# Leaving the empty slots out of a gather of expert rows

## Chip, cores and metric

The kernel runs on one core of one Trainium2 chip. Times are device microseconds (us) of one launch; the figure compared is the median of several runs of the same kernel. "MB" is a million bytes.

## The reference

One transformer-like block over 512 tokens of 2048 float32 features: a layer norm, a token mixer (eight gated DeltaNet heads beside a sliding-window attention) with one input and one output projection, a second layer norm, a mixture of experts, and a last layer norm. The change lies in the mixture of experts, which is

```
eid      = the 2 experts of each token            # of 32, inside one of 4 groups
weights  = p(group) * renormalised top-2 probability
for each expert e, for the tokens that chose it:
    hdn = silu(x @ w_gate[e]) * (x @ w_up[e])     # 2048 -> 512
    y[token] += weight * (hdn @ w_down[e])        # 512 -> 2048
```

512 tokens with two choices each make 1024 rows over 32 experts, 32 for an expert on average. Evaluating the reference on its inputs gives these counts, for experts 0 to 31: 35 47 27 28 38 35 31 35 25 10 21 26 41 40 27 16 23 24 29 31 29 48 26 32 46 34 41 41 37 26 43 32. None is over 64, and 14 of them are over 32.

## The kernel before

The first 1100 us or so compute the projections and the mixer. Then the second layer norm leaves 512 rows `r1` in SBUF, which ACT also stores to `h1_scr` in HBM, and PE makes router logits (semaphore `logits`, 2 when both parts are there).

**Routing table.** DVE works out, step by step (semaphore `rt`), where each of the 1024 choices goes in a table in HBM, `slot_rows`: 512 places for each expert, of two numbers each, a token's index and a weight. At the very start of the program POOL has filled the whole table with zeros from the tile `unused` (line 557, 559). Later POOL writes the choices into it with eight scatters (line 615), and when they have landed it reads the first `SLOTS` = 64 places of each expert into `idx_all`, twice, once for each half of the partitions (line 622). A place that no choice has filled keeps index 0 and weight 0, so it stands for token 0 with weight 0.

**Gather.** For each of the 32 experts ("block" t), POOL issues one indirect DMA (line 629), which fetches 64 rows of `h1_scr`, 8 KB each, one for each slot, into half of the tile `xb`: partitions 0 to 63 for even t and 64 to 127 for odd t. Slot s goes to partition s of the half. From t = 2 on it waits until PE has transposed the rows of block t - 2 (`xT_ps`), so at most two gathers are ahead. The tile `xb` shares its memory with `h1T`, which the router's matmuls read until `logits`.

**Weights.** An expert has 12 pieces of 1 MB (1.049 million bytes): 8 of gate and up, 4 of down. SP loads them on its own queue (line 532) into a ring of 15 slots, each as soon as PE is done with what lay there (`w_used`). The first 14 are loaded before the routing is known.

**Expert.** PE transposes the gathered rows (line 1873), multiplies with gate and up (line 1897), then with down (line 1906); ACT scales the result with the slots' weights (line 945), and PE adds it to the tokens' rows through a 0/1 matrix `place`, which DVE makes by comparing each token's number with the slots' indices `tok_all` (line 1478, PE line 1866, DVE line 1448). PE runs the combining matmuls of block t - 1 between the gate and up matmuls of block t.

Rows beyond 64 of an expert would go through a loop at the end (`left`); with the counts above it has nothing to do.

Of the kernel before, what the change touches and what calls it, by code (L numbers as in the profile page):

```python
# [32 lines left out]
S = 512  # L33
# [17 lines left out]
SLOTS = 64  # L51
# [56 lines left out]
def build(nc, x, ln0_g, ln0_b, w_in, conv_w, a_log, dt_bias, gdn_norm_w, sinks, w_o, ln1_g, ln1_b,  # L108
# [11 lines left out]
    with ctx:  # L120
        def sem(name):
            return ctx.enter_context(nc.semaphore(name))
# [16 lines left out]
        def at(name, offset, shape, dt=F32):  # L139
            size = 4 * int(np.prod(shape[1:]))  # L140
            assert offset + size <= ARENA, (name, offset + size)
            placed[name] = offset + size
            return nc.alloc_sbuf_tensor_at(name, list(shape), dt, offset=base + offset)
# [19 lines left out]
        o = GD  # L163
# [39 lines left out]
        xb = at("xb", GD + 24 * KB, [P, D])  # L203
# [10 lines left out]
        o = CN  # L214
        small = {}

        def keep(name, shape, dt=F32):
            nonlocal o
            t = at(name, o, shape, dt)
            o += (4 * int(np.prod(shape[1:])) + 31) // 32 * 32  # L220
            return t
# [28 lines left out]
        idx = keep("idx", [P, 2], I32)  # L250
        idx_all = at("idx_all", GD + 47 * KB, [P, E, 2], I32)
# [32 lines left out]
        unused = at("unused", MX, [P, 2 * E * CAP // P], I32)  # L284
# [80 lines left out]
        gathered = [sem(f"gathered{i}") for i in range(2)]  # L365
# [15 lines left out]
        def W(eng, s, n):  # L381

            if not (isinstance(n, int) and n <= 0):
                eng.wait_ge(s, n)
# [33 lines left out]
        def slot(j):  # L418

            return (1 + j) % 2  # L420
# [133 lines left out]
        @block.gpsimd  # L554
        def _(pool):

            pool.memset(unused[:, :], 0).then_inc(table_zeroed, 1)
            pool.wait_ge(table_zeroed, 1)
            pool.dma_start(slot_rows.rearrange("(p n) o -> p (n o)", p=P), unused[:, :]).then_inc(table_zero, 16)
            pool.memset(eps[:, 0:1], LN_EPS).then_inc(zero_pad, 1)  # L560
            pool.memset(eps[:, 1:2], RMS_EPS).then_inc(zero_pad, 1)
            def lo(s, sl):
                pool.wait_ge(strip_hi, s + 1)
                W(pool, strip_mm, s - 1)
                pool.tensor_tensor(wlo[sl][:, :, :].rearrange("p k n -> p (k n)"), raw[sl][:, :],  # L565
                                   whi[sl][:, :, :].rearrange("p k n -> p (k n)").bitcast(F32),
                                   ALU.subtract).then_inc(strip_lo, 1)

            lo(0, 0)
            lo(1, 1)  # L570

            def iteration(it, gdn=True, last=False):
                for j in range(4):
                    lo(4 * it + 2 + j, slot(j + 1))
                    if j == 1 and not gdn:

                        pool.wait_ge(h_stored, 16 * TT)
                        for i in range(3):
                            pool.memset(xp[i][:, 0:CONV - 1], 0.0).then_inc(zero_pad, 1)
                    if j == 0 and gdn:  # L580

                        pool.wait_ge(par_done, 1)
                        pool.wait_ge(dec_exp, it)
                        ed = T["Ed"][:, :].rearrange("p (c i) -> p c i", c=TT)
                        pool.affine_select(out=ed, in_=ed, compare_op=ALU.is_ge, fill=0.0, base=0,
                                           pattern=[[0, TT], [-1, P]], channel_multiplier=1).then_inc(dec, 1)
                        if last:
                            for i in range(3):
                                pool.wait_ge(silu[i], HEADS)
                            pool.memset(kdup[:, :, 0:P], 0.0).then_inc(kpad, 1)  # L590

            iteration(0, gdn=False)
            with pool.Fori(1, HEADS) as it:
                iteration(it)
            iteration(HEADS, last=True)
            with pool.Fori(0, 4) as m:
                for j in range(2):
                    lo(2 * m + (Q0 + 1 + j), j)
            with pool.Fori(0, 3) as nt:
                for kg_ in range(4):  # L600
                    lo(4 * nt + (O0 + 1 + kg_), kg_ % 2)
            for kg_ in range(3):
                lo(O0 + 13 + kg_, kg_ % 2)

            pool.wait_ge(ld_ln1, 80)
            pool.wait_ge(l1_norm, TT)
            pool.tensor_tensor(r1[:, TT - 1, :], r1[:, TT - 1, :], g1[:, :], ALU.mult).then_inc(h1_last, 1)
            pool.wait_ge(h1_last, 1)
            pool.tensor_tensor(r1[:, TT - 1, :], r1[:, TT - 1, :], b1[:, :], ALU.add).then_inc(h1_last, 1)

            pool.wait_ge(table_zero, 16)
            pool.wait_ge(rt, RT_DEST)
            for t in range(TT):
                for c in range(2):
                    pool.indirect_dma_start(slot_rows, bass.IndirectOffsetOnAxis(ap=rd[:, t, c:c + 1], axis=0),
                                            toki[:, t, c, :], None).then_inc(scattered, 16)
            pool.wait_ge(scattered, 16 * 2 * TT)
            pool.wait_ge(rt, RT_ALL)
            pool.wait_ge(logits, 2)
            pool.wait_ge(h1_stored, 16 * TT)  # L620
            for h in range(2):
                pool.dma_start(idx_all[SLOTS * h:SLOTS * (h + 1), :, :],
                               slot_rows.rearrange("(e c) o -> c e o", c=CAP)[0:SLOTS, :, :]).then_inc(scattered, 16)
            pool.wait_ge(scattered, 16 * 2 * TT + 32)
            for t in range(E):
                half_ = slice(SLOTS * (t % 2), SLOTS * (t % 2 + 1))
                if t >= 2:
                    pool.wait_ge(xT_ps, 2 * (t - 1))
                pool.indirect_dma_start(xb[half_, :], None, h1_scr,  # L629
                                        bass.IndirectOffsetOnAxis(ap=idx_all[0:SLOTS, t, 0:1], axis=0)).then_inc(gathered[t % 2], 16)  # L630

            r_idx = pool.alloc_register("r_idx")
            left = pool.value_load(ovi[0:1, 2 * LEFTOVER:2 * LEFTOVER + 1], min_val=0, max_val=LEFTOVER)
            with pool.If(left > 0):
                with pool.Fori(0, left) as i:
                    row = pool.value_load(ovi[0:1, bass.ds(i + LEFTOVER, 1)], min_val=0, max_val=E * CAP - SLOTS)
                    pool.wait_ge(lf_dve, LF_DVE * i + LF_START)
                    for h in range(2):
                        pool.dma_start(idx[SLOTS * h:SLOTS * (h + 1), :], slot_rows[bass.ds(row, SLOTS), :]).then_inc(lf_rows, 16)
                    pool.reg_mov(r_idx, 48 * i + 32)  # L640
                    pool.wait_ge(h1_stored, 16 * TT)
                    pool.wait_ge(lf_rows, r_idx)
                    pool.indirect_dma_start(xb[0:SLOTS, :], None, h1_scr,
                                            bass.IndirectOffsetOnAxis(ap=idx[0:SLOTS, 0:1], axis=0)).then_inc(lf_rows, 16)

            pool.wait_ge(ld_ln2, 32)
            for i, t in enumerate(POOL_TILES):
                pool.wait_ge(f_root, 2 + i)
                pool.tensor_tensor(r1[:, t, :], r1[:, t, :], b2[:, :], ALU.add).then_inc(f_done_p, 1)
# [1348 lines left out]
```

## Time and profile before

| | |
|---|---|
| median of 3 runs (lowest, highest) | 2295.27 us (2295.11, 2295.28) |
| profiled execution, its own time | 2295.32 us |
| its span in the profile | 2293.5 us |
| mean granted TensorE clock | 0.933 of full speed |
| bytes read from HBM, written | 499.92 MB, 12.72 MB |
| busy: PE, DVE, ACT, POOL | 85%, 52%, 27%, 15% of the span |

The span is what the engines' records cover; the profiled execution's own time is 1.8 us longer. An engine's busy share is an average over very different stages, so the stage around the change is read by itself.

### The profile page before, as it was taken

Reading aid. Unit: us, or ns where it says so; the run is one execution under the profiler, and the core shown is the slowest. Engines: PE = TensorE matmul, PEld = TensorE weight load, DVE = VectorE, ACT = ScalarE, POOL = GpSimd, SP = SyncE. Lnnn points to the kernel's source line nnn. Section 1 sums busy time; section 2 is a strip of 40 time slices with the busy share of each in tenths; the row PEclk is TensorE's granted clock in tenths of the full one; section 3 lists DMA queues with packets and bytes.
Section 4 is the critical chain, followed back from the end, with each engine's and each line's share of the span. In section 5 each row is a group of like instructions: output and inputs, shape, how many; then the busy total and the mean of one; then the engine's idle time right before and its main releaser. Section 6 shows DMA issues by size and latency. Waiting matters only on the chain.

```text
span 2293.5 us, 24624 instructions
## 1 busy us (share of the span) xinstructions
PE 1950.0 (85%) x9654; PEld 1218.4 (53%) x9654; DVE 1182.2 (52%) x1772; ACT 615.4 (27%) x915; POOL 355.3 (15%) x128
## 2 busy tenths in 40 slices
PE   4899999999998987899619998889889888988991
PEld 3677787778777765688513433333333333333330
DVE  6777557656664355310523554454445444544558
ACT  4224313322332354311321222212221222122211
POOL 1422222221322212144320000000000000000002
PEclk8999999999999898899869999999999999999995
DMA  5422212112212211432558999999999999999991
GB/s 182 149 72 55 55 37 73 45 47 55 69 47 56 56 55 55 139 110 91 202 154 331 392 404 395 394 394 407 391 395 402 398 394 394 407 393 391 407 392 74
DMA packets 168958, 513.75 MB, mean 224 GB/s; under 512 B 13393, under 2 KB 105745, under 8 KB 114353
## 3 DMA queue, kind: packets, MB, share of 16 engines
q1 hardware_dynamic: 165344, 491.53, 56.5%
q0 software_dynamic: 2960, 16.95, 3.2%
q10 hardware_dynamic: 576, 4.19, 0.4%
q8 instruction: 54, 0.88, 0.2%
q14 instruction: 24, 0.19, 0.0%
HBM read 499.92 MB, written 12.72 MB: 224 GB/s over the span
## 4 chain that ended last, share of the span: by engine, by line
PE 46%; DMA 30%; DVE 14%; issue 4%; ACT 3%; SPq 2%; POOL 0%; DVEq 0%; ACTq 0%
DMA ring<-in_w_up 27%; PE bank L1897 8%; PE bank L1559 7%; PE bank L1560 7%; PE bank L1561 7%; PE bank L1906 3%; PE bank L1866 2%; PE bank L1690 2%; PE bank L1687 2%; DVE half L1091 2%; PE bank L1679 2%; SPq L532 2%; DMA ring<-in_w_down 1%; DVE gd_L L1212 1%; DVE sc L1264 1%
## 5 line engine op out<-in xcount | busy, mean ns | idle before, releaser
L1897 PE MATMUL bank<-ring,xbT 128*64 128x512 f32 x2048 | 507.9, 641 | 92.5 <-DMA ring<-in_w_up 91.6
L1448 DVE TENSOR_TENSOR r<-r,bank 128x512 f32<-128x512 f32 x512 | 318.1, 681 | 249.9 <-PE bank L1866 248.1
L565 POOL TENSOR_TENSOR wlo<-raw,whi 128x2048 fp32r<-128x2048 f32 x61 | 283.1, 4641 | 700.4 <-ACT whi L678 474.1
L1897 PEld LDWEIGHTS bank<-ring,xbT 128*64 128x64 f32 x2048 | 158.0, 146 | 393.7 <-issue 392.7
L1559 PE MATMUL bank<-hTh,wlo 128*128 128x512 f32 x720 | 309.0, 429 | 20.3 <-POOL wlo L565 14.3
L1560 PE MATMUL bank<-hTl,whi 128*128 128x512 f32 x720 | 285.4, 396 | 0.0
L1561 PE MATMUL bank<-hTh,whi 128*128 128x512 f32 x720 | 285.2, 396 | 0.0
L945 ACT ACTIVATE yw<-bank,wts_all 64x512 f32<-64x512 f32 x256 | 174.8, 683 | 253.2 <-PE bank L1906 249.1
L1906 PE MATMUL bank<-ring,hidT 128*64 128x512 f32 x1024 | 227.0, 595 | 2.3 <-DMA ring<-in_w_down 1.8
L629 POOL DMA_INDIRECT xb<-h_scr,idx_all x32 | 28.8, 898 | 917.8 <-PE bank L1873 907.3
L1866 PE MATMUL bank<-yhl,place 128*128 128x512 f32 x512 | 158.2, 429 | 13.0 <-DVE r L1448 10.1
L1559 PEld LDWEIGHTS bank<-hTh,wlo 128*128 128x128 f32 x720 | 139.3, 193 | 47.2 <-issue 20.4
L1453 DVE CAST yhl<-yw 128x512 fp32r<-128x512 f32 x128 | 53.8, 421 | 200.0 <-ACT yw L945 200.0
L934 ACT ACTIVATE hid<-bank 64x512 f32<-64x512 f32 x32 | 18.9, 589 | 509.5 <-PE bank L1897 509.5
L1561 PEld LDWEIGHTS bank<-hTh,whi 128*128 128x128 f32 x720 | 137.8, 191 | 31.0
L1560 PEld LDWEIGHTS bank<-hTl,whi 128*128 128x128 f32 x720 | 139.1, 193 | 21.7 <-issue 0.7
L1906 PEld LDWEIGHTS bank<-ring,hidT 128*64 128x64 f32 x1024 | 70.6, 137 | 142.0 <-issue 138.7
L678 ACT ACTIVATE whi<-raw 128x2048 fp32r<-128x2048 f32 x53 | 101.1, 1907 | 165.3 <-PE bank L1561 165.2
L1866 PEld LDWEIGHTS bank<-yhl,place 128*128 128x128 f32 x512 | 87.5, 190 | 108.6 <-issue 89.8
L1559 PE MATMUL bank<-whi,mxl 128*128 128x512 f32 x256 | 100.5, 392 | 0.7 <-ACT mixT L845 0.7
L1560 PE MATMUL bank<-wlo,mxh 128*128 128x512 f32 x256 | 100.3, 392 | 0.0
L1561 PE MATMUL bank<-whi,mxh 128*128 128x512 f32 x256 | 100.2, 391 | 0.0
(299 smaller groups left out, 2219.9 us busy)
## 6 DMA issues: line engine op xcount, KB each, us to landing
ring<-in_w_gate SPq DMA_DIRECT2D x128, 1024.0 KB, 29.8
ring<-in_w_up SPq DMA_DIRECT2D x128, 1024.0 KB, 30.3
ring<-in_w_down SPq DMA_DIRECT2D x128, 1024.0 KB, 29.1
raw<-in_w_in SPq DMA_DIRECT2D x45, 1024.0 KB, 5.5
raw<-in_w_o SPq DMA_DIRECT2D x16, 1024.0 KB, 5.1
xt<-in_x SPq DMA_DIRECT2D x4, 1024.0 KB, 9.3
h_scr<-xt SPq DMA_DIRECT2D x4, 1024.0 KB, 4.3
r<-h_scr SPq DMA_DIRECT2D x1, 4096.0 KB, 13.8
```

The source lines that it names most:

```text
L532: sp.dma_start(ring[n % RING][:, :], weight_source(t, i)).then_inc(w_loaded[n % RING], 16)
L565: pool.tensor_tensor(wlo[sl][:, :, :].rearrange("p k n -> p (k n)"), raw[sl][:, :], whi[sl][:, :, :].rearrange("p k n -> p (k n)").bitcast ...
L678: act.activation(whi[sl][:, :, :].rearrange("p k n -> p (k n)"), raw[sl][:, :], ACT.Copy).then_inc(strip_hi, 1)
L945: i = act.activation(yw[half_, q, :], DN[j][SLOTS * h:SLOTS * (h + 1), :], ACT.Copy, scale=wts_all[half_, t:t + 1])
L1448: dve.tensor_tensor(v, v, comb_bank(q, tt)[:, :], ALU.add).then_inc(comb_done, 1)
L1453: dve.tensor_copy(yhl[:, q, :], yw[:, q, :]).then_inc(yw_split, 1)
L1559: mm(bank, lo_, rh, start=first, stop=False)
L1560: mm(bank, hi_, rl, start=False, stop=False)
L1561: return mm(bank, hi_, rh, start=False, stop=final)
L1866: mm(comb_bank(q, tt)[:, :], place[n % 2][:, tt * P:(tt + 1) * P], yhl[:, q, :], start=True, stop=True).then_inc(comb_ps, 1)
L1897: i = mm(GU[SLOTS * h:SLOTS * (h + 1), :], xT_[:, k, :], w[:, kk * F:(kk + 1) * F], start=k == 0, stop=k == KD - 1)
L1906: i = mm(DN[j][SLOTS * h:SLOTS * (h + 1), :], hidT[:, c, :], w[:, n0:n0 + F], start=c == 0, stop=c == KF - 1)
```

## The change

The table starts with index `S` = 512 in every place, one past the last token, in place of 0 (the weight stays 0); this takes two memsets with a stride in place of one. The gather of rows (and the one of the loop at the end) gets a bound: an index over `S` - 1 = 511 is left out and is no error. Such a slot's partition of `xb` then keeps what lay in it, so POOL sets the whole tile `xb` to zero once, after `logits` has reached 2 and before it waits for the scatters. `place` has no 1 for index 512, since the tokens are numbered 0 to 511. How many rows an expert has is known only on the chip, so the matmuls still work on 64 slots.

```diff
-            pool.memset(unused[:, :], 0).then_inc(table_zeroed, 1)
-            pool.wait_ge(table_zeroed, 1)
+            fields = unused[:, :].rearrange("p (n o) -> p n o", o=2)
+            pool.memset(fields[:, :, 0:1], S).then_inc(table_zeroed, 1)
+            pool.memset(fields[:, :, 1:2], 0).then_inc(table_zeroed, 1)
+            pool.wait_ge(table_zeroed, 2)
             pool.dma_start(slot_rows.rearrange("(p n) o -> p (n o)", p=P), unused[:, :]).then_inc(table_zero, 16)
...
                     pool.indirect_dma_start(slot_rows, bass.IndirectOffsetOnAxis(ap=rd[:, t, c:c + 1], axis=0),
                                             toki[:, t, c, :], None).then_inc(scattered, 16)
+            pool.wait_ge(logits, 2)
+            pool.memset(xb[:, :], 0.0).then_inc(table_zeroed, 1)
             pool.wait_ge(scattered, 16 * 2 * TT)
             pool.wait_ge(rt, RT_ALL)
-            pool.wait_ge(logits, 2)
+            pool.wait_ge(table_zeroed, 3)
             pool.wait_ge(h1_stored, 16 * TT)
...
                 pool.indirect_dma_start(xb[half_, :], None, h1_scr,
-                                        bass.IndirectOffsetOnAxis(ap=idx_all[0:SLOTS, t, 0:1], axis=0)).then_inc(gathered[t % 2], 16)
+                                        bass.IndirectOffsetOnAxis(ap=idx_all[0:SLOTS, t, 0:1], axis=0),
+                                        bounds_check=S - 1, oob_is_err=False).then_inc(gathered[t % 2], 16)
...
                     pool.indirect_dma_start(xb[0:SLOTS, :], None, h1_scr,
-                                            bass.IndirectOffsetOnAxis(ap=idx[0:SLOTS, 0:1], axis=0)).then_inc(lf_rows, 16)
+                                            bass.IndirectOffsetOnAxis(ap=idx[0:SLOTS, 0:1], axis=0),
+                                            bounds_check=S - 1, oob_is_err=False).then_inc(lf_rows, 16)
```

Between the scatters and the first gathers, POOL's program reads like this before the change (the number is the row's place in POOL's program; `x7` stands for seven alike; the waits are those added since the row above):

```order
68 L615 DMA slot_rows<-toki,rd 16384x2 [waits rt,table_zero]
69 L615 DMA slot_rows<-toki,rd 16384x2 x7
70 L622 DMA idx_all<-slot_rows 64x32x2 [waits logits,h1_stored,rt,scattered]
71 L622 DMA idx_all<-slot_rows 64x32x2
72 L629 DMA xb<-h_scr,idx_all 64x2048 [waits scattered]
73 L629 DMA xb<-h_scr,idx_all 64x2048
74 L629 DMA xb<-h_scr,idx_all 64x2048 [waits xT_ps] x30
```

And like this after it, in the lines of the changed kernel:

```order
69 L617 DMA slot_rows<-toki,rd 16384x2 [waits rt,table_zero]
70 L617 DMA slot_rows<-toki,rd 16384x2 x7
71 L620 MEMSET xb 128x2048 [waits logits]
72 L626 DMA idx_all<-slot_rows 64x32x2 [waits table_zeroed,h1_stored,rt,scattered]
73 L626 DMA idx_all<-slot_rows 64x32x2
74 L633 DMA xb<-h_scr,idx_all 64x2048 [waits scattered]
75 L633 DMA xb<-h_scr,idx_all 64x2048
76 L633 DMA xb<-h_scr,idx_all 64x2048 [waits xT_ps] x30
```

One memset has come in between the scatters and the reading of the table, and the wait on `logits` has moved to it. PE, DVE, ACT and SP keep their instructions and their order.

## Rows read from the trace of the kernel before

**Rows 1.** The page: the span in 40 equal slices (57.3 us each).

```profile
DMA  5422212112212211432558999999999999999991
GB/s 182 149 72 55 55 37 73 45 47 55 69 47 56 56 55 55 139 110 91 202 154 331 392 404 395 394 394 407 391 395 402 398 394 394 407 393 391 407 392 74
```

**Rows 2.** The page: DMA queues; packets, MB, share of 16 engines' span.

```profile
q1 hardware_dynamic: 165344, 491.53, 56.5%
q0 software_dynamic: 2960, 16.95, 3.2%
```

**Rows 3.** Waits of PE from 1200 us on: total, times, longest.

```profile
PE bank L1897 <- DMA ring<-in_w_up: 91.6, 52, 4.5
PE bank L1873 <- DMA xb<-h_scr,idx_all: 42.0, 1, 42.0
```

**Rows 4.** The chain that ended last, in order of time: start, us, what.

```profile
1178.26 9.90 DMA slot_rows<-toki,rd
...
1200.87 5.61 DMA xb<-h_scr,idx_all
1206.53 2.03 PE bank L1873 x16
...
1285.17 7.02 PE bank L1906 x32
...
1312.78 7.02 PE bank L1906 x32
...
2195.96 27.00 DMA ring<-in_w_up
2223.10 3.67 PE bank L1897 x16
```

**Rows 5.** Line 629 before 1215 us and from 1339 us: durations in ns, starts, landing.

```profile
L629 POOL DMA_INDIRECT xb<-h_scr,idx_all x3: 901/924/933, 1200.9 to 1208.8; - x3
...
L629 POOL DMA_INDIRECT xb<-h_scr,idx_all x25: 892/896/902, 1339.5 to 2136.4; - x25
DMA to landing us min/median/max: 9.0/9.5/10.3
```

**Rows 6.** Stretches: us, PE, PEld, DVE, ACT, POOL busy, PEclk, DMA share, GB/s.

```profile
1202.00:1206.00 4.00, 0.00 (x0) 0.00 (x0) 0.00 (x0) 0.00 (x0) 0.92 (x1) 0.50 0.89 203
1222.00:1232.00 10.00, 8.59 (x51) 4.15 (x48) 1.87 (x3) 2.85 (x4) 0.89 (x1) 1.00 1.01 425
1428.00:1442.00 14.00, 14.00 (x74) 6.59 (x74) 10.16 (x17) 1.57 (x3) 0.90 (x1) 1.00 1.01 421
1443.90:1447.90 4.00, 3.72 (x18) 1.01 (x14) 0.00 (x0) 0.23 (x1) 0.00 (x0) 1.00 1.05 260
1410.00:2210.00 800.00, 714.75 (x3198) 287.05 (x3196) 382.55 (x650) 172.11 (x269) 19.72 (x22) 0.95 1.01 398
2212.00:2222.00 10.00, 9.63 (x42) 3.88 (x40) 7.07 (x13) 0.20 (x1) 0.00 (x0) 1.00 1.02 421
```

**Rows 7.** POOL in order of time: start, busy us, instruction, idle before it.

```profile
1178.26 0.97 POOL L615 DMA_INDIRECT slot_rows<-toki,rd  x1 [0.30 <-issue]
1188.45 2.27 POOL L622 DMA_DIRECT2D idx_all<-slot_rows  x2 [9.22 <-DMA slot_rows<-toki,rd]
1202.11 0.92 POOL L629 DMA_INDIRECT xb<-h_scr,idx_all  x1 [0.30 <-issue]
```

**Rows 8.** POOL by line: count, busy us, mean ns, idle before.

```profile
L565 POOL TENSOR_TENSOR wlo<-raw,whi 128x2048 fp32r<-128x2048 f32 x61 | 283.1, 4641 | 700.4 <-ACT whi L678 474.1 <-ACT whi L686 226.3
L590 POOL MEMSET kdup<- 128x512 f32 x1 | 0.5, 524 | 0.0
```

**Rows 9.** The page: DMA issues; count, KB each, us to landing.

```profile
xt<-in_x SPq DMA_DIRECT2D x4, 1024.0 KB, 9.3
```

## The prediction

> **What bounds the kernel now.** I read the page's slices first. From about the 23rd slice of 40 to the 39th, some 980 us, the DMA row says 9 (over 90% of all 16 engines) at 391 to 407 GB/s, while before that it is mostly 1 to 5 [rows 1]. That stretch is the mixture of experts, and its 384 pieces of weights make 403 MB. Then the stretches: in the 800 us from 1410 us on the DMA share is 1.01 and the rate 398 GB/s [rows 6]; it is 1.01 already at 1222 to 1232 us and still 1.02 at 2212 to 2222 us. So the DMA engines have work without a gap for 1000 us, and what the transfers take there is what the stage takes. PE's waits agree: 91.6 us for `ring<-in_w_up`, 52 times; the next in size, 42.0 us, is the one wait for the first gather [rows 3]. The chain ends with a load that lands at 2223 us and then PE's last gate and up matmuls [rows 4], after which comes a tail that the change does not touch. PE could go faster: early on, with a full ring, two blocks' down matmuls start at 1285.17 and 1312.78 us, 27.6 us apart [rows 4], whereas the gathers from 1339.5 to 2136.4 us, which are 25 and so 24 blocks, come 796.9 / 24 = 33.2 us apart [rows 5].
>
> **What a gather costs.** This is the number that the case turns on. Of the loads alone the rate is 421 GB/s (1428 to 1442 us, and again at the end) [rows 6]. Twelve pieces of 1.049 MB at that rate are 12.58 / 0.421 = 29.9 us. The block takes 33.2 us, so one gather of 64 rows costs the loads 3.3 us. By its bytes it should cost 0.524 MB / 0.421 = 1.25 us. The rest is seen in the 4 us of a gather: the rate falls to 260 GB/s, the gather's own bytes included, at a DMA share of 1.05 [rows 6]. All engines are busy and move less. The gather writes to 64 of the 128 partitions only, and the first two gathers, which run with nothing beside them, show the same: 203 GB/s at a share of 0.89, half of 421 [rows 6]. So rows bound for half of the partitions go in at half the rate, and loads that share an engine with them are held up behind them.
>
> The Trainium skill (DMA: Bandwidth & Descriptors, Anatomy of one DMA) prices a transfer on this path at about 2.0 us fixed, which overlaps with others, plus its bytes over 436e3 per us: for one gather an estimate of 1.2 us of engine time, and 0.6 us saved by halving it, 17 us over 29 gathers. The rows say 3.3 us per gather, and halving that would be 48 us; I go by the rows.
>
> **The change part by part.**
>
> *Rows left out.* 1024 of 2048 rows stay [the counts with the reference]: 8.4 of the 16.95 MB of the software queue go [rows 2]. Of the 32 gathers the first three are issued before the loads fill the engines again (by 1208.8 us [rows 5]; the DMA share is full from 1222 us); the other 29 lie in the saturated stretch, and each us that they cost less is a us off the end, as long as PE's 27.6 us per block stays below the DMA's time. Even with nothing left of a gather that is 29.9, so it does.
>
> How much one gather gets cheaper depends on who carries the rows that stay. The filled slots are the first ones of the 64, since choices are numbered from 0 in each expert. The share of 0.89 with nothing but gathers on the queues [rows 6] says that all 16 engines carry rows, so four each. The loads give every engine the same amount, each load is complete only when all 16 are, so what counts is the most burdened engine. Two ways to deal the rows:
> - In order, four successive slots to an engine. The first engine has slots 0 to 3, which are filled for every expert, and the engines up to the seventh have nearly all of theirs. Their own work, 4 rows of 8 KB at 421 / 16 = 26.3 GB/s, 1.25 us, stays in full. What can go is the other 3.3 - 1.25 = 2.05 us, which came from two rows meeting at one place. Half of the rows are gone, so half of that, 1.0 us; and in the 14 of 32 experts with over 32 rows there is still a second row to meet for the first engines, which I count as no gain: 1.0 x 18/32 = 0.58 us per gather.
> - Spread, so that every engine loses half of its rows. Then half of 3.3 us goes, 1.65 us per gather.
>
> No view of the trace says which engine takes which slot, since every row is 8 KB whether filled or not. I take the first, as the plainest way to cut a list of 64 into 16 shares: 29 x 0.58 = 16.8 us. The ends are 0 and 29 x 3.3 / 2 = 48 us.
>
> The Trainium skill speaks for the first (same page, Why a DMA increments its semaphore by 16: SWDGE puts ceil(partitions/16) successive partitions on each engine for some direct copies, so that 100 partitions leave the last engine without data). It speaks of direct copies, and no row here shows it for an indirect one.
>
> *First gather.* It is on the chain: 5.61 us from 1200.87 us, then PE's transposes [rows 4]. 0.524 MB at 203 GB/s are 2.6 us of it. With 35 rows, four on an engine and alone at 26.3 GB/s, that is 1.25 us, so PE starts 1.3 us earlier, and the loads behind it too. The check of 64 indices could cost something: the gather's instruction takes 0.92 us now [rows 7]; a doubling would eat 0.9 of it. I take 1.3 us, with 0 and 2 as ends.
>
> *The memset of `xb`.* 128x512 took 524 ns on POOL, so at most four times that, 2.1 us, for 2048 columns; a subtraction of that size takes 4.64 us, the upper end [rows 8]. It comes after the last scatter, which ends at 1179.23 us, and POOL idles 9.22 us there until the scatters land [rows 7]. So it costs nothing; without that cover it would put 2.1 us on the chain, once. `logits` has long been at 2, since the scatters themselves need the routing that follows it.
>
> *The two strided memsets* at the start replace one of the same 256 columns (under 0.524 us by the row of 512 [rows 8]), and the table is needed only 1100 us later: nothing. The two `eps` memsets behind them go a fraction of a us later, and ACT needs them only when rows of x have landed, which takes 9.3 us [rows 9], and been summed.
>
> *The bound on later gathers* could lengthen their instructions, but POOL idles for most of 33 us before each, and a gather lands 9.5 us after its issue [rows 5], one block ahead of its use.
>
> **Sum.** Against the profiled execution's own 2295.32 us, 0.05 us above the median: 2295.3 - 16.8 - 1.3 = 2277.2 us.
>
> **The rivals.**
> - *The rows spread evenly over the engines.* For it: no row excludes it, and a rule that looks at the slot's number some other way than by runs of four is easy to imagine. Against it: nothing but that cutting the list into 16 runs is the simplest. 2295.3 - 48 - 1.3 = 2246 us, and up to 2262 if only part is even. Chance 0.22.
> - *Nothing is saved, because the change doesn't leave transfers out*: a slot over the bound is given a transfer of its own all the same, to some other place. For it: no row of this trace has a bounded gather. 2295.3 us, or 2294 if the first gather is a little shorter. Chance 0.12.
> - *Slower: the uneven load pulls the engines apart.* The first engines fall behind at each gather and the others run ahead until the ring's 15 pieces stop them; if the rows of the first engines then meet loads of engines that never pause for rows of their own, each row waits longer than now (8 KB at 260 / 16 = 16.3 GB/s are 0.50 us, against 0.31 us undisturbed). At a third more per gather, 1.1 us x 29 = 32 us, it would be 2295.3 + 32 - 1.3 = 2326 us; it decides once the first engines' cost is over the present 3.3 us. Against it: half of the writers to the crowded half have gone. Chance 0.05.
> - *The forecast*, 2266 to 2290 us: 0.61.
>
> The Trainium skill (same page, The descriptor swizzle) gives 128-partition transfers an engine by (partition >> 2) & 7 within 64 partitions; by that alone a 64-partition gather would lie on 8 engines, with slots s and s + 32 on the same, and skipping would relieve each. The share of 0.89 with gathers alone speaks against it here.
>
> **Numbers.** From the chances: 0.8 of the mass lies between 2251 us, into the spread case, and 2291 us, short of no change. About 0.2% (4.6 us) is what a measurement of this kernel can tell from no change. Faster by more than that: the forecast, the spread case, and a little of the third: 0.86; within it 0.09; slower 0.05.
>
> **What would show it.** In the changed profile: the software queue at some 8.6 MB in place of 16.95; 24 blocks from the eighth gather's issue on at 32.6 us each in place of 33.2; the rate in the 4 us of a gather above 260 GB/s; PE's wait for `ring<-in_w_up` down by about 15 us; and the DMA share a little below 1.01, since half of the engines have less to do. If the share stays at 1.01 and the blocks come at 31.5 us, the rows were spread. If the bytes are as before, the bound did nothing. I would be wrong upwards if PE, not the loads, took over the chain; PE at 27.6 us per block says that it does not.

## The result, and the profile after

The changed kernel takes 2255.12 us (median of 4 runs, 2253.01 to 2259.62) against 2295.28 us (2295.11 to 2296.24): a ratio of 0.9829, 95% interval 0.9816 to 0.9842, so 40 us or 1.7% off, well outside the noise. The profiled execution took 2253.29 us. I had forecast 2277.2 us.

The page of the changed kernel: the slices (56.3 us each), and the DMA queues, to be read against [rows 1, 2].

```profile
DMA  5422112112211221243266999999999999999991
GB/s 186 149 76 56 41 52 63 48 53 59 56 49 52 75 57 37 86 150 103 105 277 195 406 406 406 409 410 403 407 406 415 401 410 402 409 399 401 413 377 75
...
q1 hardware_dynamic: 165344, 491.53, 57.2%
q0 software_dynamic: 2960, 8.57, 1.7%
```

The stage is as saturated as it was, at mostly 399 to 415 GB/s in place of 391 to 407, and 8.4 MB less of it is gathered rows. The software queue moves 8.57 MB in place of 16.95, as it should, and its share of the engines' time has fallen from 3.2 to 1.7%. Its packets are still 2960: a left-out row of 8 KB has become a packet of 4 bytes (in the packet records 1024 of each size have changed places). The page's "HBM read" stays at 499.92 MB before and after, and at 499.92 MB in e2 below, which gathers nearly nothing, so it does not count these packets.

The waits of PE in the stage (to be read against [rows 3]):

```profile
PE bank L1903 <- DMA ring<-in_w_up: 71.2, 66, 4.3
PE bank L1879 <- DMA xb<-h_scr,idx_all: 39.5, 1, 39.5
```

The chain that ended last, in order of time (against [rows 4]):

```profile
1176.46 8.28 DMA slot_rows<-toki,rd
1185.03 1.15 POOL idx_all L626
1186.18 10.97 DMA idx_all<-slot_rows
1197.95 4.27 DMA xb<-h_scr,idx_all
1202.27 2.02 PE bank L1879 x16
...
2154.60 26.35 DMA ring<-in_w_up
```

From the landing of the first gather to the landing of the last load of gate and up, the last one on the chain, it was 2195.96 + 27.00 - 1200.87 - 5.61 = 1016.5 us, and is 2154.60 + 26.35 - 1197.95 - 4.27 = 978.7 us. That is 37.8 us, by far the most of the change. The first gather also lands 4.3 us earlier (1202.22 against 1206.48 us). Of these, 1.34 are its own (5.61 to 4.27); the rest comes from the scatters before it, their start and their landing, and moves as much in kernels that don't touch them (in e1 below the first gather starts at 1201.79 us, in e5 at 1198.80).

Lines 633 and 620 on POOL, in order of time, then line 633's gathers as a group, to be read against [rows 5, 7]:

```profile
1177.43 1.82 POOL L620 MEMSET xb<- 128x2048 f32 x1
1185.03 2.27 POOL L626 DMA_DIRECT2D idx_all<-slot_rows  x2 [5.78 <-DMA slot_rows<-toki,rd]
...
1394.64 0.93 POOL L633 DMA_INDIRECT xb<-h_scr,idx_all  x1 [26.66 <-PE bank L1879]
1426.79 0.94 POOL L633 DMA_INDIRECT xb<-h_scr,idx_all  x1 [31.22 <-PE bank L1879]
1456.97 0.93 POOL L633 DMA_INDIRECT xb<-h_scr,idx_all  x1 [29.24 <-PE bank L1879]
```

```profile
L633 POOL DMA_INDIRECT xb<-h_scr,idx_all x24: 931/935/939, 1367.0 to 2097.1; - x24
DMA to landing us min/median/max: 7.4/7.9/9.3
```

The memset takes 1.82 us and POOL still idles 5.78 us behind it. A gather's instruction is 0.04 us longer than before (0.935 against 0.896), which lies in POOL's idle time. The blocks come (2097.1 - 1367.0) / 23 = 31.7 us apart in place of 33.2, and a gather lands after 7.9 us in place of 9.5.

Stretches of the changed kernel (columns as in [rows 6]): the 4 us after two gathers reach the DMA engines, with 21 and 26 rows, and 760 us of the stage.

```profile
1430.90:1434.90 4.00, 3.27 (x16) 0.86 (x12) 0.00 (x0) 0.68 (x1) 0.00 (x0) 1.00 1.01 346
1461.00:1465.00 4.00, 3.59 (x18) 1.00 (x14) 0.00 (x0) 0.36 (x1) 0.00 (x0) 1.00 1.01 311
1410.00:2170.00 760.00, 691.05 (x3169) 283.71 (x3170) 381.43 (x648) 167.90 (x263) 20.56 (x22) 0.98 1.01 407
```

The rate during a gather falls to 346 and 311 GB/s where it fell to 260. The share is still 1.01: on average no engine has time without a packet in the middle of the stage. The prediction had named blocks of 31.5 us at a share of 1.01 as the sign that the rows were spread, and blocks of 32.6 us for its own case; 31.7 us is the former.

### The profile page after: what moved, and what is told of

It reads as the page before. It is cut to its first block, busy times and chain, and to the rows that moved or that the text cites. A ratio compares the mean times of both kernels' runs of the same rounds, so it can differ in the third digit from the quotient of the medians.

```text
span 2251.5 us, 24658 instructions
## 1 busy us (share of the span) xinstructions
PE 1932.4 (86%) x9654; PEld 1215.6 (54%) x9654; DVE 1183.3 (53%) x1772; ACT 615.2 (27%) x915; POOL 360.1 (16%) x130
## 3 DMA queue, kind: packets, MB, share of 16 engines
q0 software_dynamic: 2960, 8.57, 1.7%
HBM read 499.92 MB, written 12.72 MB: 228 GB/s over the span
## 4 chain that ended last, share of the span: by engine, by line
PE 46%; DMA 31%; DVE 15%; issue 4%; ACT 3%; SPq 1%; POOL 1%; DVEq 0%; ACTq 0%; POOLq 0%
DMA ring<-in_w_up 29%; PE bank L1903 8%; PE bank L1565 7%; PE bank L1566 7%; PE bank L1567 7%; PE bank L1912 3%; PE bank L1696 2%; PE bank L1872 2%; PE bank L1693 2%; PE bank L1685 2%; DVE half L1097 2%; DVE gd_L L1218 1%; DVE sc L1270 1%; SPq L532 1%; PE bank L1645 1%
## 5 line engine op out<-in xcount | busy, mean ns | idle before, releaser
L1903 PE MATMUL bank<-ring,xbT 128*64 128x512 f32 x2048 | 488.1, 620 | 72.6 <-DMA ring<-in_w_up 71.2
L1872 PE MATMUL bank<-yhl,place 128*128 128x512 f32 x512 | 159.2, 431 | 12.1 <-DVE r L1454 9.2
```

Source lines behind the costliest of these rows:

```text
L1872: mm(comb_bank(q, tt)[:, :], place[n % 2][:, tt * P:(tt + 1) * P], yhl[:, q, :], start=True, stop=True).then_inc(comb_ps, 1)
L1903: i = mm(GU[SLOTS * h:SLOTS * (h + 1), :], xT_[:, k, :], w[:, kk * F:(kk + 1) * F], start=k == 0, stop=k == KD - 1)
```

## The experiments

Theory P, formed after the result: the rows that stay are spread over the engines more evenly than I had assumed, because an engine does not take four successive slots but two pairs, slots 2e, 2e + 1 and 32 + 2e, 33 + 2e for engine e. It came from the start times of the software queue's 8 KB packets in the trace of the changed kernel. Theory F is the prediction's, four successive slots. For the gather of expert 9, which has 10 rows, these are the starts of its packets in us from the gather's issue, read from the packet records, with two later kernels beside it that are described below:

```
changed kernel  4.19 4.27 4.29 4.34 4.35 | 4.97 5.17 5.24 5.37 5.38
by fours (e9)   4.35 4.39 4.41 | 4.71 5.18 5.25 | 6.21 6.38 | 7.21 7.52
one by one(e10) 4.23 4.24 4.26 4.28 4.30 4.32 4.33 4.34 4.35 4.39
```

In the changed kernel five rows start together and five more some 0.9 us later: five engines with two rows each. By theory F it would be three engines, with four, four and two. That is what e9 shows, which was built to deal choices so: groups of 3, 3, 2 and 2. In e10, built to give every row its own engine, all ten start within 0.16 us. (The bars are mine. A row takes 0.31 us where nothing disturbs it, so there is room for a packet of the loads before the engine's next row.)

The diffs below are cut to what matters; counts in waits that change with them are left out.

**The memset alone (e1).**

```diff
+            pool.wait_ge(logits, 2)
+            pool.memset(xb[:, :], 0.0).then_inc(table_zeroed, 1)
             pool.wait_ge(scattered, 16 * 2 * TT)
             pool.wait_ge(rt, RT_ALL)
-            pool.wait_ge(logits, 2)
+            pool.wait_ge(table_zeroed, 2)
```

> The kernel before with nothing added but the memset of xb between the scatters and the reading of the table. Every theory: the memset (1.82 us in the changed kernel) lies in the 9.2 us that POOL idles there, so no change, 2295.3 us within 1. If it weren't hidden, 2297.

Measured: 2295.49 us (10 runs), ratio 0.9998 (0.9986 to 1.001). The interval reaches from -3.2 to +2.3 us, which by itself would not exclude the memset's 1.8 us. The trace of e1 does: POOL idles 6.54 us behind the memset until the scatters have landed, so it is hidden.

```profile
1180.95 1.82 POOL L618 MEMSET xb<- 128x2048 f32 x1
1189.32 2.28 POOL L624 DMA_DIRECT2D idx_all<-slot_rows  x2 [6.54 <-DMA slot_rows<-toki,rd]
```

**All rows left out (e2).**

```diff
-                                        bounds_check=S - 1, oob_is_err=False).then_inc(gathered[t % 2], 16)
+                                        bounds_check=0, oob_is_err=False).then_inc(gathered[t % 2], 16)
```

> The changed kernel with the bound at 0, so that all rows but those of token 0 are left out (the experts then work on zeros for the others). Theory A, a left-out slot costs the DMA engines nothing: the block falls from 31.7 us to the 29.9 us of its loads alone, 29 x 1.8 = 53 us off the changed kernel, about 2202 us. Theory B, an empty slot still costs an engine a turn: with 4 on each engine at, say, 0.1 us, the block stays at 30.3 us, about 2214 us.

Measured: 2202.02 us (2201.47 to 2202.84), ratio 0.9592 (0.9576 to 0.9609). Theory A holds: a left-out slot costs the engines nothing that can be seen. Its page shows the stage at the rate of loads alone:

```profile
GB/s 190 153 77 39 57 57 57 57 38 66 48 41 81 39 65 50 39 182 96 76 281 83 400 421 420 420 420 421 421 421 421 420 421 420 421 421 420 421 380 76
DMA packets 168957, 497.00 MB, mean 226 GB/s; under 512 B 15438, under 2 KB 107790, under 8 KB 116398
...
q0 software_dynamic: 2960, 0.20, 0.4%
```

This kernel is the floor for the rest: what the others take above 2202.0 us, over 29 gathers, is what a gather costs. For the kernel before it is (2295.3 - 2202.0) / 29 = 3.2 us, close to the 3.3 us of the prediction, which was read from the blocks' distance. (The kernels' starts differ too, and that is in it. The first gather lands at 1202.25 us in e2 and at 1206.48 in the kernel before, which makes 0.15 us per gather. By the stage alone, from that landing to the landing of the last load of gate and up, 926.9 us in e2 and 1016.5 before, a gather costs 3.1 us.)

**Two dealings of 32 rows (e3, e4).** Both have the same number of rows, the same bytes and the same groups of four partitions; only the engines differ, if theory P is right. The diff is that of e3; e4 has `(0, 1)` in place of `(0, 2)`.

```diff
-            pool.memset(fields[:, :, 0:1], S).then_inc(table_zeroed, 1)
+            pool.memset(fields[:, :, 0:1], 0).then_inc(table_zeroed, 1)
...
+            pool.memset(idx_all[:, :, :], S).then_inc(table_zeroed, 1)
...
             for h in range(2):
-                pool.dma_start(idx_all[SLOTS * h:SLOTS * (h + 1), :, :],
-                               slot_rows.rearrange("(e c) o -> c e o", c=CAP)[0:SLOTS, :, :]).then_inc(scattered, 16)
+                for first in (0, 2):
+                    pool.dma_start(idx_all[SLOTS * h + first:SLOTS * (h + 1):4, :, :],
+                                   slot_rows.rearrange("(e c) o -> c e o", c=CAP)[first:SLOTS:4, :, :]).then_inc(scattered, 16)
```

> Exactly 32 rows in every gather: the table starts with index 0 as before, but idx_all is preset to the index out of bounds and only slots 0, 2, 4, ... 62 of each expert are loaded into it (choices in odd places are left out of the result; two more small DMAs in the start, some 2 us). Theory P, an engine has slots 2e, 2e+1, 32+2e and 33+2e: two rows on every engine, half of the 3.3 us go in 29 gathers, 2295.3 - 48 - 1.3 + 2.3 = 2248 us. Theory F, an engine has four successive slots: two rows on every engine too, the same 2248 us.

> As the one with even slots, and again exactly 32 rows in every gather, but slots 0, 1, 4, 5, 8, 9, ... 60, 61. Theory P: eight engines have four rows and the other eight none; the loads wait for the eight, as in my forecast for four successive slots, so 0.6 to 1 us less than 3.3 per gather, 2268 to 2279 us. Theory F: two rows on every engine, as with the even slots, 2248 us.

Measured: 2245.05 us (2243.03 to 2245.39), ratio 0.9776 (0.9758 to 0.9794), for the even slots; 2269.19 us (2268.47 to 2270.36), ratio 0.9884 (0.9867 to 0.9902), for the paired ones. 24 us between them with equal bytes: theory F, which gives both the same, falls. A gather costs 1.5 us with two rows on every engine, and 2.3 us with four on eight engines. Both figures flatter a little: the reading of the table lands after 4.62 us in these two in place of 11, so the first gather lands at 1198.1 us, 4 us earlier than in e2, where I had added 2.3 us. By the stage alone (974.9 and 998.9 us against 926.9) it is 1.7 and 2.5 us, and the difference of 24 us stays. How the loads end shows the engines pulled apart. Paired slots:

```profile
2185.00:2195.00 10.00, 9.64 (x42) 3.91 (x41) 7.08 (x13) 0.38 (x1) 0.00 (x0) 1.00 0.86 357
2195.00:2205.00 10.00, 6.91 (x32) 2.74 (x32) 5.86 (x11) 0.98 (x2) 0.00 (x0) 1.00 0.46 192
2205.00:2211.00 6.00, 5.76 (x28) 1.72 (x24) 0.96 (x2) 0.19 (x1) 0.00 (x0) 1.00 0.19 78
```

Even slots:

```profile
2165.00:2175.00 10.00, 9.62 (x44) 3.90 (x41) 7.07 (x13) 0.00 (x0) 0.00 (x0) 1.00 1.02 421
2175.00:2185.00 10.00, 8.59 (x42) 3.26 (x40) 4.29 (x8) 0.97 (x2) 0.00 (x0) 1.00 0.71 295
```

With the paired slots some half of the engines are done 10 us and more before the others (a share of 0.46 over 10 us, then 0.19); with the even slots the share is full until nearly the end. (The last transfers are the two parameter rows of the last layer norm, dealt to all engines alike.) The loads' semaphores say the same. Each rises in sixteen steps, which I take for the sixteen engines' shares. These are the steps of the very last weight load, in us from its first step, read from the semaphore records:

```
even (e3)    0.0 0.2 0.7 0.8 0.9 2.6 2.9 5.4 6.0 6.4 6.4 6.8 6.8 6.9 8.7 9.4
paired (e4)  0.0 0.1 0.2 0.2 0.3 0.9 1.6 1.6 | 11.2 11.3 12.1 13.7 17.1 17.4 17.8 19.9
```

Eight steps come within 1.6 us, and the other eight 11 to 20 us after the first: eight engines against eight, as theory P has it. Over the middle of the stage (loads from 1500 to 2100 us) the median distance from the first step to the sixteenth is 5.2 us in e2, 5.8 in the kernel before, 6.4 with the even slots, 8.8 in e10, 13.2 in the changed kernel, and 21.0 with the paired slots and in e9. What is read as a wait for `ring<-in_w_up` is a wait for the fullest engine's part of it.

**Dealt by fours, and one by one (e9, e10).** Here all rows are gathered, and the order in which the table's places are loaded into the slots is changed so that, by theory P, an engine gets four successive choices (e9), or choice j goes to engine j modulo 16 (e10). The diff is that of e9; e10 reads places `32 * c + 16 * b` to `32 * c + 16 * b + 15` in the last line.

```diff
             for h in range(2):
-                pool.dma_start(idx_all[SLOTS * h:SLOTS * (h + 1), :, :],
-                               slot_rows.rearrange("(e c) o -> c e o", c=CAP)[0:SLOTS, :, :]).then_inc(scattered, 16)
+                for c in range(2):
+                    for b in range(2):
+                        pool.dma_start(idx_all[SLOTS * h + 32 * c + b:SLOTS * h + 32 * c + 32:2, :, :],
+                                       slot_rows.rearrange("(e c) o -> c e o", c=CAP)[2 * c + b:SLOTS:4, :, :]).then_inc(scattered, 16)
```

> The changed kernel, all rows gathered, but the table's places are loaded into the slots in an order that gives each DMA engine (by theory P) four successive choices, which is what my prediction assumed: the first engine then has 128 of the run's 1024 rows. Six more small DMAs of 1.15 us at the start, some 7 us on the chain. Theory P: the prediction's sum for this dealing, 2277, plus 7, so 2275 to 2284 us. If it isn't the fullest engine that decides, as in the changed kernel plus 7: 2262 us.

> The same with the same DMAs at the start, but choice j goes to a slot of engine j modulo 16 (by theory P), so the fullest engine has 76 of 1024 rows in place of 92 in the changed kernel. Theory P: somewhat less than the changed kernel plus 7, 2252 to 2260 us, and about 20 us less than dealt by fours. If the dealing doesn't matter: both kernels the same.

Measured: 2289.12 us (10 runs, 2284.13 to 2292.68), ratio 0.9976 (0.9967 to 0.9986), by fours; 2250.65 us (2249.7 to 2251.41), ratio 0.9813 (0.9796 to 0.9829), one by one. 38 us between two kernels that do the same transfers. The 7 us that I had added for more DMAs at the start were wrong: the two parts of the chain, issue and landing, add up to the same. Without them the range for e10 would have been 2245 to 2253 us, and it lies there; whether it is faster than the changed kernel's 2255.1 us is left open by the two intervals, which overlap. The chain by fours:

```profile
1185.87 4.43 POOL idx_all L628 x7
1190.31 6.94 DMA idx_all<-slot_rows
1198.08 5.27 DMA xb<-h_scr,idx_all
```

4.43 + 6.94 = 11.4 us, against 1.15 + 10.97 = 12.1 in the changed kernel. So e9, 5 us over the range that I had given for it, is 12 us over its top once those 7 us are taken off (2268 to 2277), and that matters: a gather costs (2289.1 - 2202.0) / 29 = 3.0 us there, hardly less than the 3.2 of 64 full rows. Two 4 us stretches of its gathers, with 21 and 26 rows:

```profile
1438.30:1442.30 4.00, 3.29 (x16) 0.86 (x12) 0.00 (x0) 0.66 (x1) 0.00 (x0) 1.00 1.02 297
1471.50:1475.50 4.00, 3.62 (x18) 1.01 (x14) 0.00 (x0) 0.34 (x1) 0.00 (x0) 1.00 1.05 236
```

**Another place to start for half of the experts (e5).**

```diff
-    r[:, E:2 * E] = (np.arange(E) * CAP)[None, :]
+    r[:, E:2 * E] = (np.arange(E) * CAP + 16 * (np.arange(E) // 2 % 2))[None, :]
```

> The changed kernel, but in 16 of the 32 experts (2, 3, 6, 7, ...) the first choice goes to slot 16 in place of slot 0, by another constant in the routing table; with these counts all still fit in 64 slots, while in general up to 48 only would. Theory P: with pairs of slots on an engine, the first engine has 92 of the run's 1024 rows in the changed kernel and the last 32; its 92 rows cost 29 x 1.8 = 53 us in the stage. Here the fullest engine has about 75, so some 10 us less, about 2245 us. If it isn't the fullest engine that counts but the number of rows alone: no change, 2255 us.

Measured: 2258.35 us (2256.23 to 2258.76), ratio 0.984 (0.9823 to 0.9856). A miss: no gain (the interval overlaps the changed kernel's). Counted through, the fullest engine has 82 rows here and not 75, against 92 in the changed kernel (and the last one there 34, not 32), and half of that gain should still be 5 us. The run's count of rows on the fullest engine is thus not the law. Another count fits: taking in each gather its own fullest engine and adding up, it is 92 rows in both kernels, 76 in e10 and 128 in e9. That this is the law, and why an engine's light gathers should not make up for its full ones, no run shows; and e4, with 128 by this count too, is 20 us faster than e9. Who writes to which partitions beside it was changed too. This stays open.

**Rows dealt to all 128 partitions (e6, e7, e8).** The price of 3.3 us in place of 1.25 was put down to the gather's writing to 64 partitions. Here each row goes as two halves of 4 KB to partitions s and s + 64.

```diff
-    gate_v = w_gate[0].rearrange("e (p k) f -> p e k f", p=P)
+    gate_v = w_gate[0].rearrange("e (h p k) f -> p e h k f", h=2, p=P)
...
-                half_ = slice(SLOTS * (t % 2), SLOTS * (t % 2 + 1))
+                half_ = slice(D // 2 * (t % 2), D // 2 * (t % 2 + 1))
...
-                pool.indirect_dma_start(xb[half_, :], None, h1_scr,
-                                        bass.IndirectOffsetOnAxis(ap=idx_all[0:SLOTS, t, 0:1], axis=0)).then_inc(gathered[t % 2], 16)
+                pool.indirect_dma_start(xb[:, half_], None, h1_scr.rearrange("s (h c) -> (s h) c", h=2),
+                                        bass.IndirectOffsetOnAxis(ap=idx2[:, t:t + 1], axis=0)).then_inc(gathered[t % 2], 16)
...
+            for h in range(2):
+                dve.tensor_scalar(idx2[SLOTS * h:SLOTS * (h + 1), :], idx_all[SLOTS * h:SLOTS * (h + 1), :, 0:1].rearrange("p e o -> p (e o)"),
+                                  2.0, float(h), ALU.mult, ALU.add).then_inc(slots_ready, 1)
```

(`up_v` and the pieces' source change like `gate_v`, still 8 KB in a run for each partition; PE transposes features 0 to 1023 from partitions 0 to 63 and the others from 64 to 127, 16 transposes as before.)

> The kernel before with all 64 slots gathered, but each row of 8 KB goes as two of 4 KB to partitions s and s + 64, so that a gather writes to all 128 partitions (the weights' rows are dealt to the partitions in another order to fit; two small DVE operations make the indices, about 1 us at the start). Theory of the meeting: of the 3.3 us a gather keeps only its own 1.25 us, 29 x 2.05 = 59 us off, 2295.3 - 59 - 1 + 1 = about 2236 us. Theory that a row from the software queue is slow in itself, whatever it writes to: 2295 us, or more, as there are twice as many rows.

> The changed kernel with the gather to all 128 partitions. No meeting and half of the bytes: a gather costs 0.65 us if evenly dealt, 0.9 us if the fullest engine has 92 of 1024 again; 29 x 2.4 to 2.65 = 70 to 77 us off the kernel before, 2218 to 2226 us. It can't come under the 2202 us of the kernel that leaves all rows out. If rows of the software queue are slow in themselves: as the changed kernel, 2255 us.

> The one before with 16 experts' first choice in slot 16. If the fullest engine counts there too, up to 29 x 0.2 = 6 us less than it, about 2215 us; if dealing over 128 partitions is even anyway or 16 slots further fall to the same engines, no difference.

Measured:

| kernel | us | ratio to the kernel before |
|---|---|---|
| e6, all 64 slots, 128 partitions | 2238.51 (2237.46 to 2241.54) | 0.9758 (0.9742 to 0.9774) |
| e7, with rows left out | 2222.47 (2221.16 to 2225.58) | 0.9684 (0.9668 to 0.97) |
| e8, e7 with the start at 16 in half of the experts | 2219.18 (2216.18 to 2222.08) | 0.9676 (0.9659 to 0.9692) |

e6 and e7 are where they were expected, e8 is 4 us above. A gather of 64 full rows costs (2238.5 - 2202.0) / 29 = 1.26 us now, which is the 1.25 us of its bytes. The page of e6, and two stretches in the middle of its gathers:

```profile
GB/s 187 150 76 57 40 53 63 49 49 64 55 40 63 76 38 56 32 204 95 50 345 166 421 420 420 421 420 421 421 420 420 421 421 420 421 420 420 421 375 75
```

```profile
1425.40:1429.40 4.00, 4.00 (x20) 1.15 (x16) 0.00 (x0) 0.00 (x0) 0.00 (x0) 1.00 1.01 414
1456.70:1460.70 4.00, 4.00 (x20) 1.15 (x16) 0.00 (x0) 0.00 (x0) 0.00 (x0) 1.00 1.03 418
```

414 and 418 GB/s where the kernel before has 260 [rows 6], with all the rows still there: the slowness was the crowding on half of the partitions, and neither the software queue nor the number of rows. The edit halves the gather's packets too, from 8 KB to 4 KB, but their size is not it: the loads' own packets are 8 KB and last 0.31 us each (median over the stage). While a gather runs they last 0.54 us on average in the kernel before and 0.31 in e6 (packet records). Nor is it that every empty slot reads token 0's row, since e6 still does that. This alone, without leaving anything out, is faster than the change (2238.5 against 2255.1 us), and with the change it gives 2222.5 us, 73 us off the kernel before. e8's interval overlaps e7's, and its table holds only 48 rows in half of the experts, so e7 is the version to keep.

## Why the prediction was wrong

- **What bounds it** was right: the saturated DMA engines for 1000 us. All that the experiments took off the gathers came off the end, down to 2202 us with next to none left.
- **A gather's price**, 3.3 us against 1.25 by its bytes, was right (3.2 against the floor), and so was its cause, shown by e6. The Trainium skill's 2.0 us plus bytes / 436e3 (DMA: Bandwidth & Descriptors, Anatomy of one DMA) holds here for the bytes' part only where a gather writes to all partitions: an estimate of 1.2 us by it, against 1.26 measured in e6 and 3.2 in the kernel before.
- **The step that failed** is the one that I named as unseen in the trace: "four successive slots to an engine". The runs show pairs (e3 against e4, the loads' steps in e4, and the packets' starts in the changed kernel and in e9). With pairs, an expert of up to 32 rows leaves at most two on any engine, so nearly half of the price goes, which is the rival of rows spread over the engines: 2246 us "and up to 2262 if only part is even", chance 0.22. Measured 1.83 us per gather, 1.4 less than before, for 29 gathers 40 us (the first gather's 1.3 among them).
- **The sum for that dealing was off too.** I had 0.58 us per gather for fours, 16.8 us in all. e9, which makes it so, is 6.2 us under the kernel before, 1.3 of them for the first gather perhaps, so at most 0.2 us per gather. The wrong term is "half of the rows are gone, so half of" the meeting. The four rows on an engine of e9's gather (10 rows in the list above) start from 4.4 to 7.2 or 7.5 us, about 1.0 us apart, even with three engines writing, and a packet of the loads between two of them takes 0.31 us undisturbed. So a row costs the fullest engine an estimated 0.7 us there; by the kernels' times it is 3.0 / 4 = 0.75 us in e9 and 3.2 / 4 = 0.8 before. It is not the same everywhere: e4, too, has four rows on eight engines and pays only 2.3 / 4 = 0.6. e4 writes to two of every four neighbouring partitions of the half, e9 to all four of some and none of others, and the loads' packets last 0.47 us on average during e4's gathers and 0.55 during e9's (packet records). That the neighbours make this difference is not tested. Two errors, which partly cancelled: with the right law and the wrong dealing I would have said 2290 us, and with the right dealing 2246 to 2262.
- **First gather**: 5.61 to 4.27 us, 1.34 off, forecast 1.3. The closeness is luck in part: e9 has the dealing that the working assumed, and there it takes 5.27 us, only 0.34 less than before. **Memset** hidden: the trace of e1; 1.82 us long, within the bound of 2.1. **Strided memsets**, **bound on later gathers**: nothing seen in the time.
- **"The DMA share a little below 1.01"** was wrong: it is 1.01. Engines with fewer rows can run ahead in their queue, but a load lands some 29 us after its issue, and that much lead is soon used up: in e4, where eight engines have no rows at all, the share is 1.01 as well, at 400 GB/s from 1410 to 2110 us. So the share does not tell how the rows are dealt, and the packets of the engines that are ahead must last longer instead; what makes them is open. The end shows the dealing, below. Behind the chain's last load, which lands at 2180.95 us, four loads of down still land, the last at 2190.8. That one's first step comes 18.4 us before its sixteenth, against 9.0 us in the kernel before: some engines are done with everything, the two parameter rows too, while others still carry weights (share 0.97, then 0.48).

The end of the loads in the changed kernel:

```profile
2165.00:2175.00 10.00, 8.87 (x39) 3.41 (x38) 4.62 (x8) 5.47 (x8) 0.00 (x0) 1.00 1.01 419
2175.00:2185.00 10.00, 9.45 (x40) 3.65 (x39) 7.01 (x12) 0.22 (x1) 0.00 (x0) 1.00 0.97 405
2185.00:2195.00 10.00, 8.60 (x40) 3.20 (x40) 3.57 (x6) 0.95 (x3) 0.00 (x0) 1.00 0.48 202
```

- **The rule for the shares.** The Trainium skill (DMA: Bandwidth & Descriptors, Why a DMA increments its semaphore by 16) gives some direct copies ceil(partitions/16) partitions on each engine. Four on each is what this indirect gather has as well, but the page does not say which four; "successive" was my reading, and the runs show two pairs. The formula of the Trainium skill (same page, The descriptor swizzle) is for a transfer to 128 partitions; carried over to 64 it would put the ten rows above on three engines, and the trace shows five.

## What to carry to other kernels

When DMA bounds a stage, price a small transfer by what the rate does while it runs, not by its bytes: this one cost 2.5 times its bytes, and spreading it over all 128 partitions won more than halving it. When a change takes rows out of a transfer, ask which engine loses them, since a load is complete only with the engine that is furthest behind; the same 1024 rows took 2250.7 or 2289.1 us by the order of the slots alone. And when a forecast hangs on a mapping that no view shows, give both answers near even chances.

## What was not expected of the hardware

- A slot over the bound is not dropped but becomes a packet of 4 bytes: the software queue has 2960 packets before and after, in e2 too, while the packets under 512 B of the whole program go from 13393 (e6 has 13392) to 15438 in e2. Some 2045 more of them cost nothing that can be seen (420 to 421 GB/s in the stage).
- For an indirect DMA to 64 partitions, an engine takes two successive slots of the first 32 and two of the second.
- How much a kernel varies from run to run differs: 1.4 us from lowest to highest in four runs of e2 and 1.7 in four of e10, but 6.6 in four of the changed kernel, 8.6 in ten of e9 and 8.7 in thirteen of the kernel before. I have no cause for it.
